# Stick attention without staging and with one mask, and a last layer on 260 of 272 tokens

## The reference, cut to what matters

```
k_sh, v_sh = kvn @ sb_wk, kvn @ sb_wv          # all 272 tokens
q = rms_norm(h) @ sb_wq
# per head (16 heads of 64): z = q.k / 8, valid where key < query
log_1m    = where(valid, log_sigmoid(-z), 0)
log_after = cumsum(log_1m, reversed over keys) - log_1m
w         = where(valid, exp(log_sigmoid(z) + log_after), 0)
h = h + (w @ v) @ sb_wo
h = h + conv_glu_ffn(rms_norm(h), ...)         # up to 5632, causal conv of width 3, silu(gate) * val, down
return rms_norm(h, final_norm_g)[:, 16:, :]
```

## Time and profile before

| what | us |
|---|---|
| three runs | 1553.12, 1558.01, 1563.17 (median 1558.01) |
| the profiled execution | 1562.59 |
| its span | 1560.8, so 1.8 around it |
| mean granted clock of TensorE | 0.959 |

### The profile page before, as it was taken

The page is one execution under the profiler, slowest core; times in us unless marked ns, Lnnn a source line. Parts: engine busy times, 40 slices in busy tenths (PEclk is TensorE's granted clock), DMA queues, the critical chain, the costliest instruction groups (busy, mean ns, idle before and its releaser), DMA issues.

```text
span 1560.8 us, 30115 instructions
## 1 busy us (share of the span) xinstructions
PE 1466.6 (94%) x12742; PEld 1322.8 (85%) x12742; DVE 897.8 (58%) x1783; ACT 328.3 (21%) x657; POOL 32.0 (2%) x47
## 2 busy tenths in 40 slices
PE   7999999989999969998889999999998889999997
PEld 6888788889999836777787999989998778999997
DVE  2141133347864481466554777886685546887865
ACT  1132104140000111420112122220101652222201
POOL 0130000000000000000000000000001100000000
PEclk9999999999999989999998999999998668999999
DMA  8434244246544402321000344444443002444442
GB/s 338 152 122 158 68 148 149 97 126 205 176 174 163 162 0 99 118 70 42 4 4 2 112 139 155 162 146 173 169 162 135 1 1 96 147 162 152 147 163 81
DMA packets 54479, 190.42 MB, mean 122 GB/s; under 512 B 6961, under 2 KB 9137, under 8 KB 53970
## 3 DMA queue, kind: packets, MB, share of 16 engines
q1 hardware_dynamic: 50480, 180.67, 33.7%
q10 hardware_dynamic: 3874, 7.92, 1.6%
HBM read 187.51 MB, written 1.05 MB: 121 GB/s over the span
## 4 chain that ended last, share of the span: by engine, by line
PE 87%; DVE 8%; issue 3%; ACT 1%; DMA 0%; POOL 0%; DVEq 0%; ACTq 0%; SPq 0%; PEldq 0%; POOLq 0%
PE ps L1799 86%; DVE arena L1551 1%; DVE arena L1574 1%; DVE arena L1602 1%; DVE arena L1717 0%; DMA ring<-in_stream 0%; DVE rs L2255 0%; DVE arena L1601 0%; DVE arena L792 0%; DVE arena L1721 0%; DVE arena L790 0%; DVE arena L1340 0%; DVE arena L1332 0%; DVE res L2264 0%; DVE arena L1330 0%
## 5 line engine op out<-in xcount | busy, mean ns | idle before, releaser
L1799 PE MATMUL ps<-arena,ring 128*128 128x136 f32 (+3 forms) x4816 | 864.0, 333 | 18.0 <-DMA ring<-in_stream 8.1
L1799 PEld LDWEIGHTS ps<-arena,ring 128*128 128x128 f32 x4816 | 752.0, 193 | 103.1 <-issue 19.9
L1799 PE MATMUL ps<-arena 64*64 64x64 f32 (+8 forms) x6748 | 572.0, 263 | 45.9 <-DVE arena L1730 12.2
L1799 PEld LDWEIGHTS ps<-arena 64*64 64x64 f32 (+3 forms) x6748 | 504.1, 165 | 88.0 <-issue 44.6
L790 DVE TENSOR_TENSOR arena<-ring 128x512 f32<-128x512 f32 x92 | 63.3, 688 | 95.1 <-PE ps L1799 93.6
L1799 PE MATMUL ps<-arena,consts 128*128 128x16 f32 (+10 forms) x384 | 90.4, 391 | 8.5 <-DVE arena L1721 4.8
L1551 DVE SCALAR_TENSOR_TENSOR arena<-arena,cols 128x271 f32<-128x271 f32 (+1 forms) x176 | 84.0, 498 | 11.2 <-ACT arena L1226 8.1
L1799 PEld LDWEIGHTS ps<-arena,consts 128*128 128x128 f32 (+3 forms) x384 | 70.5, 231 | 22.2 <-DVE arena L1721 4.9
L777 ACT COPY arena<-ps 128x136 f32<-128x136 f32 (+1 forms) x64 | 17.2, 268 | 323.1 <-PE ps L1799 323.1
L1226 ACT ACTIVATE arena<-arena,cols 128x272 f32<-128x272 f32 x88 | 49.2, 606 | 125.0 <-DVE arena L1484 70.3
L792 DVE TENSOR_TENSOR arena<-arena,ring 128x512 f32<-128x512 f32 x92 | 63.7, 693 | 3.2
(11 more groups left out here) (270 smaller groups left out, 896.6 us busy)
## 6 DMA issues: line engine op xcount, KB each, us to landing
ring<-in_stream SPq DMA_DIRECT2D x342, 512.0 KB, 3.7
consts<-in_consts ACTq DMA_DIRECT2D x1, 1580.0 KB, 8.7
arena<-in_x_t ACTq DMA_DIRECT2D x1, 1024.0 KB, 5.8
arena<-in_mem_t ACTq DMA_DIRECT2D x1, 1024.0 KB, 4.8
res<-in_x_t ACTq DMA_DIRECT2D x1, 1024.0 KB, 14.6
out_t<-arena SPq DMA_DIRECT2D x4, 256.0 KB, 2.5
arena<-in_g ACTq DMA_DIRECT2D x1, 640.0 KB, 5.8
arena<-in_w ACTq DMA_DIRECT2D x2, 256.0 KB, 4.7
```

Source lines behind the costliest of these rows:

```text
L1799: return nc.tensor.matmul(out, lhs, rhs, start=start, stop=stop)
```

## The change

- Staging goes: the score products read kT and qT, the transposes read vT. POOL has no part any more, and `kst`, `vs2`, `qst` and the memsets are gone. Key blocks have 128, 128 and 16 rows (KW).
- One mask: -1e30 in zs only. ll is max(zs, 0) from SBUF, Abs reads zs instead of PSUM, and the three products with "strict" are gone.
- The hardware loop is written out. The score products come before the transposes. The copy of the turned values moves from ACT to DVE. The output copy moves ahead of the addition on DVE. There are three ee buffers.
- `keep_busy` issues matmuls whose result nobody reads (240 columns, into the free end of bank 6): 10 once, between the scores and the transposes of unit 1, and 4 before the output products of units 6 and 7.
- The queries, sb_o, ffb_up, ffb_down and the last norm leave out the first 12 tokens (K0 = META - 4), so they run on L2 = 260: halves of 130 columns, and 260 + 144 + 16 = 420 columns of scores for a head.

```diff
+        K0 = META - 4
+        L2 = L - K0
+        def tokens(name):
+            return slice(K0 if name in ("sb_q", "sb_o", "ffb_up", "ffb_down", "ffb") else 0, L)
+        def compact(buf):
+            n = buf.shape[1]
+            return buf.rearrange("p n t -> p (n t)")[:, 0:n * L2].rearrange("p (n t) -> p n t", n=n)
...
-                              ("sb_q", Seven(FIRST["sb_q"], T2, [4], (4, 0), WIDE, 0, 4, GB, False), 1),
+                              ("sb_q", Seven(FIRST["sb_q"], L2 // 2, [4], (4, 0), WIDE, 0, 4, GB, False), 1),
...
-        ZW = L + (L - P) + META
-        kst, vs2, qst = four.take(2, 384), four.take(2, 384), four.take(2, L)
-        zs, ll, ee = [[four.take(2, ZW) for _ in range(2)] for _ in range(3)]
+        Q0 = [K0, P, 2 * P]
+        ZW = sum(L - q for q in Q0)
+        zs, ll, ee = [[four.take(2, ZW) for _ in range(n)] for n in (2, 2, 3)]
...
-        ZC = [0, L, L + L - P]
+        ZC = [0, L2, L2 + L - P]
+        KW = [P, P, META]
...
-                            last = mm(gps(3 + 4 * (s % 2)), ring[:, b % RING, k * P:(k + 1) * P], hf[:, k, :],
-                                      k == 0, k == KT - 1)
+                            at = tokens(name)
+                            last = mm(gps(3 + 4 * (s % 2), L - at.start), ring[:, b % RING, k * P:(k + 1) * P],
+                                      hf[:, k, at], k == 0, k == KT - 1)
...
+        def keep_busy(pe, mm, n):
+            for _ in range(n):
+                mm(ps[:, 6, L:512], const("ones"), consts[:, 0:512 - L])
+        def z_products(pe, mm, u):
             b = u % 2
-            unit(pe, k_staged, u, it)
-            unit(pe, k_vk, u - 1, it)
-            unit(pe, k_zr, u - 2, it)
-            for n in range(3):
-                last = nc.tensor.transpose(ps[:, 7, n * P:(n + 1) * P], vs2[:, b, n * P:(n + 1) * P], ident)
-            last.then_inc(k_vt, 1)
+            if u >= 2:
+                pe.wait_ge(k_zr, u - 1)
             for i in range(3):
                 for p in range(2):
                     r = slice(64 * p, 64 * p + 64)
-                    last = mm(ps[:, 2 * b + p, ZC[i]:ZC[i] + L - i * P], kst[r, b, i * P:(i + 1) * P],
-                              qst[r, b, i * P:L])
+                    last = mm(ps[0:KW[i], 2 * b + p, ZC[i]:ZC[i] + L - Q0[i]], kT[r, u, i * P:i * P + KW[i]],
+                              compact(qT)[r, u, Q0[i] - K0:L2])
             last.then_inc(k_z, 1)
+            if u == 1:
+                keep_busy(pe, mm, 10)
+            if u >= 1:
+                pe.wait_ge(k_vk, u)
+            for n in range(3):
+                last = nc.tensor.transpose(ps[0:KW[n], 7, n * P:(n + 1) * P], vT[:, u, n * P:n * P + KW[n]], ident)
+            last.then_inc(k_vt, 1)
...
+            if t + 1 < KT:
+                z_products(pe, mm, t + 1)
+            if 0 <= u < KT:
+                pe.wait_ge(k_vk, u + 1)
+                if u >= 1:
+                    pe.wait_ge(k_od, u)
+                if u >= KT - 2:
+                    keep_busy(pe, mm, 4)
+                pe.wait_ge(k_w, u + 1)
...
+        def stick_scalar(act, f, t):
+            if t < KT:
+                e = ee[t % 3]
+                act.wait_ge(k_zr, t + 1)
+                if t >= 3:
+                    act.wait_ge(k_o, t - 2)
+                f(e, zs[t % 2], ACT.Abs).then_inc(k_abs, 1)
+                act.wait_ge(k_abs, t + 1)
+                f(e, e, ACT.Exp, scale=-1.0).then_inc(k_exp, 1)
+                act.wait_ge(k_exp, t + 1)
+                f(e, e, ACT.Ln, bias=one_c).then_inc(k_ln, 1)
+            if 1 <= t <= KT:
+                act.wait_ge(k_arg, t)
+                f(ee[(t - 1) % 3], zs[(t - 1) % 2], ACT.Exp).then_inc(k_w, 1)
...
+        def stick_vector(dve, t, tt, stt, ts, cpv):
+            b, c, e = t % 2, (t - 1) % 2, ee[t % 3]
+            if t < KT:
                 z = ps[:, 2 * b:2 * b + 2, 0:ZW]
+                dve.wait_ge(k_z, t + 1)
+                if t >= 2:
+                    dve.wait_ge(k_w, t - 1)
+                for i in range(3):
+                    q0 = Q0[i] - i * P
+                    at = slice(ZC[i], ZC[i] + KW[i] - q0)
+                    stt(out=zs[b][:, :, at], in0=z[:, :, at], scalar=0.125, in1=over(const("strict_neg")[:, q0:KW[i]], 2),
+                        op0=ALU.mult, op1=ALU.add)
+                for i in range(2):
+                    at = slice(ZC[i] + KW[i] - (Q0[i] - i * P), ZC[i + 1])
+                    last = ts(zs[b][:, :, at], z[:, :, at], 0.125, None, ALU.mult)
+                last.then_inc(k_zr, 1)
+                dve.wait_ge(k_zr, t + 1)
+                ts(ll[b], zs[b], 0.0, None, ALU.max).then_inc(k_l1, 1)
+                dve.wait_ge(k_vt, t + 1)
+                if t >= 2:
+                    dve.wait_ge(k_o, t - 1)
+                cpv(vk2[:, b], ps[:, 7, 0:3 * P].rearrange("p (a b) -> p a b", a=3)).then_inc(k_vk, 1)
+            if t >= 2:
+                dve.wait_ge(k_o, t - 1)
+                cpv(compact(oT)[:, t - 2, :], ps[:, 6, 0:L2]).then_inc(k_od, 1)
+            if 1 <= t <= KT:
+                dve.wait_ge(k_sfx, t)
+                tt(zs[c], zs[c], ps[:, 4:6, 0:ZW], ALU.add).then_inc(k_arg, 1)
+            if t < KT:
+                dve.wait_ge(k_ln, t + 1)
+                dve.wait_ge(k_l1, t + 1)
+                stt(out=ll[b], in0=ll[b], scalar=-1.0, in1=e, op0=ALU.mult, op1=ALU.subtract).then_inc(k_l, 1)
```

More of the change, by code:

```diff
@@ L447, in program @@
                         for n in range(2)]
-        SRC = {"down": act_up4, "ffa_down": act2_4, "ffb_down": act2_4}
+        uu_of, cu_of, act2_of = [{"ffa": x, "ffb": compact(x)} for x in (uu, cu, act2)]
+        SRC = {"down": act_up4, "ffa_down": act2_4,
+               "ffb_down": act2_of["ffb"].rearrange("p (k b) t -> p k b t", b=2)}
         for names in (XSUM, WSUM, QUADS):
@@ L460, in program @@
         assert at + 8 * T2 <= width
-        for n, (name, x) in enumerate((("rw_o", bb), ("sb_k", hf), ("sb_v", hf), ("sb_q", hq), ("sb_o", oT), ("ffa_up", hf), ("ffb_up", hf))):
+        for n, (name, x) in enumerate((("rw_o", bb), ("sb_k", hf), ("sb_v", hf), ("sb_q", hq[:, :, K0:L]), ("sb_o", compact(oT)),
+                                       ("ffa_up", hf), ("ffb_up", hf[:, :, K0:L]))):
             SRC[name] = x.rearrange("p (k b) t -> p k b t", b=2)
@@ L683, in total_of @@
                 pe.wait_ge(sq_added, i + 1)
-                mm(gps(bank), const("mean"), sqb[:, 0, :], True, False)
+                at = slice(K0 if i >= 2 else 0, L)
+                mm(gps(bank, L - at.start), const("mean"), sqb[:, 0, at], True, False)
                 pe.wait_ge(res_sq, 8 * i + 8)
-                mm(gps(bank), const("mean"), sqb[:, 7, :], False, True).then_inc(summed, 1)
+                mm(gps(bank, L - at.start), const("mean"), sqb[:, 7, at], False, True).then_inc(summed, 1)
             def ffn(name, i, before):
@@ L730, in second_tensor @@
             pe.wait_ge(ev["sb_q"], GB + 8)
-            stick_units(pe, lambda t, it: stick_tensor(pe, mm, t, it))
+            for t in range(KT + 2):
+                stick_tensor(pe, mm, t)
             pe.wait_ge(k_od, KT)
             pe.sem_inc(ev["sb_o"], GB)
-            tiles("sb_o", FIRST["sb_o"], 2, oT, L)
+            tiles("sb_o", FIRST["sb_o"], 2, compact(oT), L2)
             seven_products(pe, mm, "sb_o")
@@ L1199, in second_scalar @@
                     keep_first_product(act, name, i)
-            stick_units(act, lambda t, it: stick_scalar(act, f, t, it))
+            for t in range(KT + 2):
+                stick_scalar(act, f, t)
             residual_scalar(act, f, "sb_o", ("ffn_g", 8), seven=1)
@@ L1210, in residual_scalar @@
                 act.wait_ge(ev[name], SEVEN[name].off + j + 1)
-                f(sqb[:, j, :], res[:, j, :], ACT.Square).then_inc(res_sq, 1)
-                f(hf[:, j, :], res[:, j, :], ACT.Copy, scale=col(gain[0], gain[1] + j)).then_inc(res_scaled, 1)
+                at = tokens(name)
+                f(sqb[:, j, at], res[:, j, at], ACT.Square).then_inc(res_sq, 1)
+                f(hf[:, j, at], res[:, j, at], ACT.Copy, scale=col(gain[0], gain[1] + j)).then_inc(res_scaled, 1)
         def ffn_scalar(act, f, root, name, layer, which):
-            root(4, L, which=which)
+            root(4, L - tokens(name).start, which=which)
+            uu, cu = uu_of[name], cu_of[name]
             wc = COLS["conv_w"] + layer * 3 * 2 * F2 + 2 * 2 * F2
@@ L1435, in quads_to_res @@
                 q = QUADS[name][i % 2]
-                p1, u2, u3, u4 = [q[:, n, :] for n in range(4)]
-                e, o = [[res[:, 2 * i + r, h * y.t:(h + 1) * y.t] for h in range(2)] for r in range(2)]
+                p1, u2, u3, u4 = [q[:, n, 0:y.t] for n in range(4)]
+                t0 = tokens(name).start
+                e, o = [[res[:, 2 * i + r, t0 + h * y.t:t0 + (h + 1) * y.t] for h in range(2)] for r in range(2)]
                 pr = lambda p: product_at(y, i, p)
@@ L1483, in quads_scaled @@
```

(7 more changed lines are left out.)

163 lines of the change are left out of this document (36 added, 127 removed).

## The result

The changed kernel takes 1535.3 us (median of four runs, 1529.8 to 1540.5) against 1560.3 for the kernel before on the same chip (median of four): a ratio of 0.9845, 95% interval 0.9809 to 0.9881. That is 24.9 us less where 27.5 were forecast. Run again later it gave 1534.7, ratio 0.9868 (0.9808 to 0.9927).

A forecast was written before the change was run, and what follows sets the result against it. TensorE, busy 94% of the span, was taken as the bound, with idle waits and half clock in the stick stage. Pairs 14.7, start 0.4, end 0.7 + 2.5, tokens 9.2: 27.5 us off 1558.0, so 1530; range 1520 to 1545.

The forecast's parts named there:

- Tokens, 9.2 us: Last layer on 260 tokens in place of 272: shorter records and steps save 9.2 us, ends 3.8 and 11.
- Rival D: Last layer: the tokens bring nothing, because 130 columns run as 136; 9 us back, 1539 us; chance 0.07.
- sb_o at full clock, 2.5: sb_o starts at full clock, where its first 6.0 us ran at half: up to 3.0 us less, 2.5 taken.
- Start and end, 0.4 and 0.7: Stick stage: first exponential gains 0.4 us; from the last exponential to sb_o the output products save 0.7.
- ScalarE's ring, 7.7 us at full clock: Stick stage: masks, Abs, exponentials, loads and logarithm form a chain that sets 7.7 us a pair at full clock.
- The period, 8.0 us: Stick stage: 8.0 us a pair in place of 10.1, ends 7.4 and 10.0; seven pairs give 14.7 us.
- to fall in some: Stick stage: clock holds in most pairs, falls in some; where briefly, 1.4 us of slack takes up part.
- A: Stick stage: the clock goes on falling; 9.4 us a pair, total 1542, or 1547 at two thirds; chance 0.27.
- C: Stick stage: the pairs stop overlapping, 12.7 us a pair, total 1563 us; chance 0.04.
- signs of being right: Exponentials 8 us apart, ScalarE idle 1.3 us before Abs, clock over 0.85, outputs released by ACT, sb_o without 0.45 us records.
- B: Stick stage and last layer: clock stays full, 7.7 us a pair, 130 columns cost as 128; 1526 us; chance 0.12.

The follow-up runs named there:

- all_tokens: The changed kernel with the last layer on all 272 tokens again: 1551.6 us, ratio to the kernel before 0.9956.
- fill_first: The changed kernel with 7 more unread matmuls before the output products of pair 0: 1539.5 us, ratio to the kernel before 0.9881.
- fill_all: The changed kernel with unread matmuls before every pair's output products (7 for pair 0, 2 for pairs 1 to 5, 4 for the last two): 1535.3 us.
- rows128: The changed kernel with the third key block on 128 rows in scores, transposes, suffix sums and outputs: 1533.4 us, ratio to the kernel before 0.9830.
- suffix128: The changed kernel with 128 rows for the third key block in the suffix sums alone: 1545.3 us in one run.

## Why the prediction was right, and which steps were not

- **Tokens, 9.2 us:** right in the sum: 8.5 in the two profiles (1.0 at sb_q, 7.5 behind it against all_tokens) and about 10 without a further fall. The cadence at 130 columns was the end that I did not take: 111.7 ns as for 128, not 112.7. Against that, the end of the up projection has 2.09 us of idle TensorE before the weight sums of ffb_down [the row at 1457.40], in place of 1.70, and after it the clock fell for 3.4 us, which costs 1.7. Rival D is out.
- **sb_o at full clock, 2.5:** right. 10.4 - 7.5 = 2.9 us; its first 8 us run at clock 1.00 (the row at 1275.04: 40 records in 8.1 us; the first 40 took 11.5 before).
- **Start and end, 0.4 and 0.7:** the end was 0.7 (2.85 us from the last exponential to sb_o against 3.55); the start gave 1.2 (the first exponential 19.85 us after the last query product, not 21.09). keep_busy ended 10.9 us after the last query product, some 2 to 4 us sooner than I had it, before the first suffix sums could start, so it cost nothing.
- **ScalarE's ring, 7.7 us at full clock:** right, 7.8, with the idle time before Abs (1.42) and its releaser as named. Its parts on VectorE were right within 0.05 us.
- **The period, 8.0 us:** here the forecast failed. It was 9.1 and 9.4, so the pairs gave 6.7 and 4.7 us, not 14.7. Two things in it were wrong. First, "to fall in some" pairs, briefly: the clock stood at half for 27.3 us on end. I worked out the idle stretch of a steady pair (1.8 us; it came to 0.78, for the longer suffix sums fill it) but not of pair 0, where ScalarE has the extra loads that I had myself counted: 3.0 us. fill_first and fill_all show these stretches as the cause. Second, the suffix sums were taken at the durations of 128-row products (3.2 and 6.4 us); with 16-row records among them they are 4.4 and 7.9 (rows128, suffix128). At half clock a pair takes 12.4 us, not 11.1, and the 1.5 us more of suffix sums cover that. By this, about 3 of the 9.1 us by which the first three periods exceed 8.0 each are the suffix sums (an estimate, two cold pairs at 1.5), and the rest is the clock.
- **Rivals and signs:** what happened in the stage is A's mechanism, at nearly A's price (9.1 and 9.4 us a pair against 9.4). Its total of 1542 was not reached because sb_o kept the full clock, which A had given up. C did not happen: 12.4 us pairs look like it, but TensorE was busy 26.3 of 27.1 us in them. Of my signs of being right the granted clock (0.82, not over 0.85) and the 8 us between exponentials did not come; the releasers and sb_o's records did. My chances had slips: forecast, B, D and half of A sum to 0.83, not 0.84, and C's 1563 lies within 1% of 1558, so 0.03 for slower has little ground.
- **The total:** the changed kernel's 1535.3 lies 5 us above the 1530 and inside the range. The 20.1 us of the profiles are 7.4 short of the sum, almost all of it the pairs' 8.0; the medians' 24.9 lie between, and no stage that the change touches shows the 4.8 us above 20.1. That the total came so near, with the largest term less than half of the forecast, is in part luck.

The clock rule that was cited from the Trainium skill ("TensorE: Matmul & The Clock Gate", section "HAM oscillation — how this bites in real kernels"), waits that throw the array back to half clock, was the better guide here than my weighing of it: the falls went on, and filling the waits ended the long ones. The page has its loop fall in every turn; here the clock also held, for the last four pairs of the changed kernel.

## What to carry to other kernels

Work out the idle stretches of the first turn of a pipeline apart from the steady one: it has other waits, and a clock that falls there is paid for over several turns. When two rings are within a few tenths of each other, relieve both, and fill what TensorE idle time is left; relieving one left the full-clock period at 7.6 to 7.8 us here, both and the fills took the stage from 87 to 71 us. Count the idle time anew after each such edit: a shorter product on TensorE leaves more of it if the period doesn't follow. And look for chains that close over two turns. Cutting the rows of a small block to what is needed can cost time: look at the cadence of the stream around it, not at the size of the one product.
